# Gathering the sparse rows of a PEER down-projection: from a laid copy, or straight from the weights

## What is computed

```
act = gelu(h . u_table[e])            # for the 128 experts e of the token
w   = softmax gate * act
y   = sum over the 128 picks of  w * v_table[e]
```

## Time and profile before

| | before |
|---|---|
| median of 3 runs | 3961.21 us |
| span of the profiled execution | 3962.2 us |
| TensorE busy | 98% of the span |
| VectorE busy | 72% |
| ScalarE busy | 34% |
| GpSimd busy | 57% |
| granted TensorE clock, mean | 0.998 |

### The profile page before, as it was taken

The page is one execution under the profiler, slowest core; times in us unless marked ns, Lnnn a source line. Parts: engine busy times, 40 slices in busy tenths (PEclk is TensorE's granted clock), DMA queues, the critical chain, the costliest instruction groups (busy, mean ns, idle before and its releaser), DMA issues.

```text
span 3962.2 us, 59722 instructions
## 1 busy us (share of the span) xinstructions
PE 3896.8 (98%) x21569; PEld 3382.9 (85%) x21569; DVE 2842.4 (72%) x3796; ACT 1330.7 (34%) x1577; POOL 2273.4 (57%) x1162
## 2 busy tenths in 40 slices
PE   6999999999999999999999999999999999999998
PEld 5788888888887888888999999999987888888886
DVE  7555555566623459997777777777537999999998
ACT  3233233342213322234444444444323333333332
POOL 6343344434442345446877777788107788787771
PEclk9999999999999999999999999999999999999999
DMA  6555555543442326687888888875549999999994
GB/s 239 189 198 198 198 192 187 194 160 138 159 167 72 117 85 244 234 279 230 243 240 239 239 239 244 245 224 139 192 178 355 375 387 390 383 391 374 391 383 190
DMA packets 385875, 943.27 MB, mean 238 GB/s; under 512 B 104136, under 2 KB 186072, under 8 KB 319736
## 3 DMA queue, kind: packets, MB, share of 16 engines
q1 hardware_dynamic: 177624, 593.08, 41.3%
q0 software_dynamic: 88064, 176.47, 14.2%
q10 hardware_dynamic: 120096, 172.59, 12.6%
HBM read 846.85 MB, written 263.97 MB: 280 GB/s over the span
## 4 chain that ended last, share of the span: by engine, by line
PE 45%; issue 31%; POOL 14%; DVE 7%; DVEq 1%; ACT 1%; DMA 1%; POOLq 1%; SPq 0%; ACTq 0%
POOL wlo L772 13%; PE bank L1670 8%; PE bank L1672 8%; PE bank L1671 8%; PE bank L1728 5%; PE bank L1730 5%; PE bank L1729 5%; DVE wlo L1757 2%; DVE res L2395 2%; PE bank L1389 1%; PE bank L1391 1%; PE bank L1390 1%; ACT whi L1358 1%; DVE res L2414 1%; DVEq L2412 1%
## 5 line engine op out<-in xcount | busy, mean ns | idle before, releaser
L772 POOL TENSOR_TENSOR wlo<-raw,whi 128x1024 fp32r<-128x1024 f32 x296 | 768.7, 2617 | 995.1 <-ACT whi L954 463.6
L834 POOL DMA_INDIRECT gates_d<-sel_g,place_u x384 | 754.9, 1966 | 209.9 <-DMA gates_d<-sel_g,place_u 120.0
L1389 PE MATMUL bank<-h_hi,whi 128*128 128x512 f32 x1712 | 674.4, 394 | 1.9 <-POOL wlo L772 1.3
L1391 PE MATMUL bank<-h_hi,wlo 128*128 128x512 f32 x1712 | 666.9, 390 | 0.0
L1390 PE MATMUL bank<-h_lo,whi 128*128 128x512 f32 x1712 | 666.3, 389 | 0.0
L1728 PE MATMUL bank<-whi,ew_hi 128*128 128x512 f32 x1408 | 550.1, 391 | 14.6 <-DVE wlo L1757 14.6
L1730 PE MATMUL bank<-whi,ew_lo 128*128 128x512 f32 x1408 | 548.5, 390 | 0.0
L1729 PE MATMUL bank<-wlo,ew_hi 128*128 128x512 f32 x1408 | 548.5, 390 | 0.0
L1670 PE MATMUL bank<-h_hi,p_hi 128*128 128x256 f32 x1600 | 452.9, 283 | 0.4 <-DVE p_lo L1757 0.4
L1671 PE MATMUL bank<-h_lo,p_hi 128*128 128x256 f32 x1600 | 452.8, 283 | 0.0
L1672 PE MATMUL bank<-h_hi,p_lo 128*128 128x256 f32 x1600 | 452.8, 283 | 0.0
(11 more groups left out here) (336 smaller groups left out, 7991.9 us busy)
## 6 DMA issues: line engine op xcount, KB each, us to landing
raw<-in_weights SPq DMA_DIRECT2D x338, 1024.0 KB
v_rows_d<-in_weights ACTq DMA_DIRECT2D x96, 1024.0 KB
x_raw<-in_weights SPq DMA_DIRECT2D x50, 1024.0 KB
parts_d<-in_weights SPq DMA_DIRECT2D x32, 1024.0 KB
v_rows_d<-in_weights SPq DMA_DIRECT2D x32, 1024.0 KB
gates_d<-zeros SPq DMA_DIRECT2D x32, 768.0 KB, 10.4
act_d<-mt ACTq DMA_DIRECT2D x128, 192.0 KB
act_in<-act_d SPq DMA_DIRECT2D x64, 384.0 KB
```

What stands on the lines that cost most here:

```text
L772: pool.tensor_tensor(wlo[slot][:, part], raw[slot][:, part], whi[slot][:, part].bitcast(F32), ALU.subtract).then_inc(lo_made, 1)
L834: pool.indirect_dma_start(out=places_d, out_offset=bass.IndirectOffsetOnAxis(ap=place_u[:, t, k:k + 1], axis=0), in_=sel_g[:, t, k:k + 1], ...
L1389: pe.matmul(bank[:, :], whi[slot][:, cols], rhs_hi[:, c, :], start=c == 0, stop=False)
L1391: last = pe.matmul(bank[:, :], wlo[slot][:, cols], rhs_hi[:, c, :], start=False, stop=c == DC - 1)
```

## The change

`parts_d` is dropped. `lay_parts` and its 32 DMAs go, as does the third DMA of `store_acts`. The part rows are gathered from `weights` itself, where the 512 numbers of an expert's quarter lie together; the index table `part_u` is computed to point there. The activations of tile 2 are gathered as single elements from `act_d`, where they lie already for the dense product, by a new `gather_part_act(k)` straight into `w_c[:, k]`, with an index table `pact_u` of its own. `pick_part` goes; `add_part` multiplies `w_c` by the gates once for every 8 picks.

```diff
-        def lay_parts(queue, sbn):
-            queue.dma_start(parts_d[bass.ds(sbn, 1), :, :, 0:512].rearrange("a i p n -> p (a i) n"),
-                            weights[bass.ds(AT_V + 4 * sbn + C_PART, 1), :, :].rearrange("a p (i n) -> (a p) i n", i=4)
-                            ).then_inc(rows_laid, 16)
...
                     if b % 2 == 1:
                         lay_rows(sp, i, b // 2)
-                    else:
-                        lay_parts(sp, 4 * i + b // 2)
...
-            parts = parts_d.rearrange("a i p n -> (a i p) n")
+            parts = weights.rearrange("a p (i n) -> (a p i) n", n=512)
+            part_cells = act_d.rearrange("a p b t -> (a p b t)").unsqueeze(1)
...
+            def gather_part_act(k):
+                pool.indirect_dma_start(out=w_c[:, k:k + 1], out_offset=None, in_=part_cells,
+                                        in_offset=bass.IndirectOffsetOnAxis(ap=pact_u[:, k:k + 1], axis=0)
+                                        ).then_inc(pact_landed, 16)
...
-            pool.wait_ge(rows_laid, 16 * (N_V + SB))
+            pool.wait_ge(rows_laid, 16 * N_V)
...
             for k in range(8):
                 gather_act(k)
+                gather_part_act(k)
...
                     if k % 8 == 0:
                         pool.wait_ge(act_landed, 16 * (k + 8))
+                        pool.wait_ge(pact_landed, 16 * (k + 8))
                     gather_act(k + 8)
+                    gather_part_act(k + 8)
...
-                act.dma_start(parts_d[bass.ds(j, 1), s, :, 512:].rearrange("a p t -> (a p) t"),
-                              mt[s % 2][:, T_PART * P:SD]).then_inc(act_stored[s % 2], 16)
...
+            dve.scalar_tensor_tensor(part_f[:, :], pos_af[:, T_PART, :], float(3 * 4 * P), place_f[:, T_PART, :],
+                                     ALU.mult, ALU.add)
+            dve.drain()
+            dve.tensor_scalar(part_f[:, :], part_f[:, :], float((AT_V + C_PART) * 4 * P), None, ALU.add)
...
-            def pick_part():
-
-                k = len(parts_added)
-                if k == PICKS:
-                    return
-                dve.wait_ge(part_landed[k % ROWS], 16 * (k // ROWS + 1))
-                dve.scalar_tensor_tensor(picked[:, :], part_row[k % ROWS][:, 512:], gate_c[:, k:k + 1], ident[:, :],
-                                         ALU.mult, ALU.mult, accum_out=w_c[:, k:k + 1])
-
             def add_part():
                 k = len(parts_added)
                 if k == PICKS:
                     return
-                dve.drain()
+                if k % 8 == 0:
+                    dve.wait_ge(pact_landed, 16 * (k + 8))
+                    at = slice(k, k + 8)
+                    tt(w_c[:, at], w_c[:, at], gate_c[:, at], ALU.mult)
+                dve.drain()
+                dve.wait_ge(part_landed[k % ROWS], 16 * (k // ROWS + 1))
                 at = res[:, T_PART, 512 * C_PART:512 * (C_PART + 1)]
-                dve.scalar_tensor_tensor(at, part_row[k % ROWS][:, 0:512], w_c[:, k:k + 1], at, ALU.mult, ALU.add
+                dve.scalar_tensor_tensor(at, part_row[k % ROWS][:, :], w_c[:, k:k + 1], at, ALU.mult, ALU.add
                                          ).then_inc(part_used, 1)
```

More of the change, by code:

```diff
@@ L50 @@
 ROW_EXTRA = PART_EXTRA = (1, 3, 4, 6, 7, 9, 10, 12)
-PART_W = 512 + P
 PICKS = RH * TOPK
@@ L271, in build_trunk @@
     place_u = sb("place_u", [P, TD, PICKS], c_at + 18 * kb, U32)
-    part_f = sb("part_f", [P, PICKS], c_at)
+    part_f = sb("part_f", [P, PICKS], c_at + 20 * kb)
     act_in = [sb(f"act_in{k}", [P, 4, SD], a_at + (32 + 12 * k) * kb) for k in range(2)]
@@ L309, in build_trunk @@
     cell_u = w("cell_u", [P, PICKS], 67.5, U32)
+    pact_u = w("pact_u", [P, PICKS], 67, U32)
     gate_p = w("gate_p", [P, PICKS], 68)
@@ L314, in build_trunk @@
     part_u = w("part_u", [P, PICKS], 76.25, U32)
-    part_row = [w(f"part{i}", [P, PART_W], 30 + 2.5 * i) for i in range(ROWS)]
+    part_row = [w(f"part{i}", [P, 512], 30 + 2 * i) for i in range(ROWS)]
     end_hi = whi + [sb("whi2", [P, SL], a_at + 32 * kb, F32R)]
@@ L407, in build_trunk @@
     rows_laid, tables_made = sm("rows_laid"), sm("tables_made")
+    pact_landed = sm("pact_landed")
     act_landed, row_used = sm("act_landed"), sm("row_used")
@@ L641, in _ @@
             for h in range(2):
-                sp.wait_ge(act_stored[h], 48 * 8 + 16)
+                sp.wait_ge(act_stored[h], 32 * 8 + 16)
             sp.wait_ge(prod_done, ALL_PRODUCTS)
@@ L696, in _ @@
             for h in range(2):
-                sp.wait_ge(act_stored[h], 48 * (EB // 2) + 16)
+                sp.wait_ge(act_stored[h], 32 * (EB // 2) + 16)
             for J in range(PAIRS - 2):
@@ L862, in _ @@
             for h in range(2):
-                pool.wait_ge(act_stored[h], 48 * (EB // 2) + 16)
+                pool.wait_ge(act_stored[h], 32 * (EB // 2) + 16)
             for k in range(8):
                 gather_act(k)
+                gather_part_act(k)
             for k in range(PICKS):
@@ L1218, in expert_out @@
                 act.wait_ge(mt_turned, N_Q + 2)
-                act.wait_ge(act_stored[s % 2], 48 * (2 * j + s // 2) + 16)
+                act.wait_ge(act_stored[s % 2], 32 * (2 * j + s // 2) + 16)
                 act.activation(mt[s % 2][:, :], banks[s % 2][:, :], ACT.Gelu_apprx_tanh).then_inc(evac, 1)
@@ L1281, in block_out @@
                 act.wait_ge(outs_added, 14 * g + 7 * h + (21, 20)[i])
-                act.wait_ge(act_stored[i], 48 * (U_PLAIN // 2 + 2 * g + h) + 16)
+                act.wait_ge(act_stored[i], 32 * (U_PLAIN // 2 + 2 * g + h) + 16)
                 act.activation(mt[i][:, :], (c_1, c_2)[i][:, :], ACT.Gelu_apprx_tanh).then_inc(e_made, 1)
@@ L2221, in _ @@
             dve.tensor_copy(gate_c[:, :], sel_g[:, T_PART, :])
-            dve.scalar_tensor_tensor(part_f[:, :], sel_i[:, T_PART, :], float(NK), sel_j[:, T_PART, :], ALU.mult, ALU.add)
             dve.drain()
+            dve.tensor_copy(pact_u[:, :], place_u[:, T_PART, :])
             dve.tensor_copy(part_u[:, :], part_f[:, :]).then_inc(tables_made, 1)
@@ L2429, in _ @@
                     add_row()
-                    pick_part()
                 low_part(J, 1)
```

2 lines of the change are left out of this document (removed).

## The result

The kernel after takes 4122.50 us, median of 4 runs (4117.54 to 4131.57), against 3962.45 us for the kernel before (4 runs, 3960.39 to 3964.01). The ratio is 1.0406, with a 95% interval of 1.0393 to 1.0419: slower by 160 us. The forecast was slower by 111 us, 4073 us, with a range of 4000 to 4150. The direction and the place were foreseen, and the size came out 49 us short.

The account below looks back on a forecast made before the run. TensorE bounds the kernel before; with a fourth gather GpSimd was to bound the down-projection. 3006 us plus 120 picks of 7.9 us, plus issue and landing, puts pick 120 at 3961, 111 us late: 3962.2 + 111 = 4073 us, range 4000 to 4150.

Parts of the forecast that it names:

- the 0.2 us per pick that were put in: GpSimd in the down-projection: waiting for activations to land, once in eight picks, costs 0.2 us per pick (25.3 / 125).
- the 3006 of the sum: Start of the down-projection: with 16 activation gathers in place of 8, the first part gather goes out at 3006 us.
- 2.98 gathers done; the remaining 1.02: Down-projection, per pick: 2.98 gathers at 2.15 us fit in VectorE's 6.6 us of work; 1.02 more cost 1.25 us each.
- 7.9 us per pick: Down-projection: GpSimd's pace with four gathers, 6.6 + 1.3 us, above TensorE's 7.22; limits kept are 7.3 and 8.8.
- two of the signs: Profile after, down-projection: TensorE's waits for `wlo` grow from 14.6 to about 110 us; VectorE's for `row` or `part` 100 to 150.
- the two fast cases: The rivals "GpSimd keeps up" (3947 us, chance 0.08) and "no difference" (3961 us, chance 0.04), left out of the range.
- half of the second: Half of the good-interlocking case: 7.3 us per pick in the down-projection, 4001 us, chance 0.14; the range starts at 4000.
- most of the third's: Most of the case without cheap gathers: 8.8 us per pick in the down-projection, 4181 us, chance 0.11; the range ends at 4150.
- GpSimd keeps up: Rival: GpSimd needs at most 7.22 us per pick in the down-projection, TensorE's 14.6 us of waits come back: 3947 us, chance 0.08.
- no difference: Rival: GpSimd keeps up in the down-projection, TensorE's waits stay as they come from ScalarE's rounding: 3961 us, chance 0.04.
- No cheap gathers: Rival: VectorE's idle time falls where GpSimd waits for activations anyway; 8.8 us per pick in the down-projection, 4181 us, chance 0.11.
- The gathers interlock well: Rival: VectorE's short operations let two gathers through; 7.3 us per pick in the down-projection, 4001 us, chance 0.14.

Follow-up runs that it names:

- e8_laid_copies_back: The kernel after with the 32 laying DMAs and the third activation store put back, unused: 4112.72 us, ratio to the kernel before 1.0377.
- e3_before_plus_gather: The kernel before with one more single-element gather per pick, its result unused: 4127.91 us, ratio to the kernel before 1.0420.
- e9_rows_of_4_kb: The kernel after with row gathers of 1024 numbers in place of 2048, the addition still at full length: 4085.68 us, ratio to the kernel before 1.0308.
- e5_ring_76: The kernel after with GpSimd's descriptor ring at 1216 bytes in place of 1024: 4071.75 us, ratio to the kernel before 1.0275.
- e2_no_fourth_gather: The kernel after without `gather_part_act`, the parts weighted with the gates squared: 3952.96 us, ratio to the kernel before 0.9976.

## Why the prediction came out as it did

**Right: the place and the mechanism.** The stages before 2975 us stayed as they were, the stage's first gather went out at 2974.57, and the laying was worth nothing (`e8_laid_copies_back`). GpSimd became the bound by the fourth gather alone (`e3_before_plus_gather`). Its price is not in the bytes: row gathers of 8 KB and element gathers alike take 0.94 us at their shortest, and rows of half the length leave the mean as it is (`e9_rows_of_4_kb`). VectorE came to wait for rows and TensorE for `wlo`.

**Right with a longer ring, in part by luck: the pace.** The forecast had (7.9 - 0.2) / 4 - 0.30 = 1.63 us for a gather in the mean; the kernel after shows 1.62. I measure the pace from the issue of the first pick's row gather to that of pick 120. In `e5_ring_76` these are 3007.19 and 3952.49 us: 945.3 / 119 = 7.94 us per pick against the forecast 7.9, and 4072 us in all against 4073. The forecast describes a kernel with room in its ring. Some of that closeness is luck. `e5_ring_76` still has some 13 us of ring gaps in mid-stage that no term stood for, 0.1 us per pick, and its waits for activations are 12.6 us, half of the 0.2 us per pick that were put in: the two cancel. Its stage also began 5.5 us before the 3006 of the sum. And the mean of 1.62 us comes from another mix: of the gathers in the stretch of the earlier trace rows 19% took 1 us or less, and the step "2.98 gathers done; the remaining 1.02" makes that about 40% in the new kernel (0.19 x 2.98 + 1.02 = 1.59 of 4), where it shows 31%. The others were shorter than before, 1.94 us in the mean and not 2.07.

In the kernel after the first part gather, at 3003.53, came 2.5 us sooner than said. From the row addition of pick 120, at 4006.15, to the end the kernel after takes 110.9 us, where 112.4 were taken over from the earlier trace rows.

**The term that was mis-sized: "7.9 us per pick" in the sum.** In the kernel after the same two issues are at 3009.30 and 3999.14 us, which is 8.32 us per pick. The step that made it, "In VectorE's 6.6 us of work GpSimd gets (6.6 - 0.2) / 2.15 = 2.98 gathers done; the remaining 1.02 cost 1.25 us each", gives every gather its duration and 0.30 us of issue, and nothing for room. In the trace, from the first part gather (3003.53) to the row addition of pick 120 (4006.15) the kernel after takes 1002.6 us, where the sum had 3961 - 3006 = 955. These 47.6 us, less the 2.5 and some 1.5 by which the start and the end were shorter, are the 44 us by which the profiled execution passed 4073. The other 5.5 us of the 49 are no step of the sum: the median of the four runs lies that far above the profiled execution, which took 4117.0 us. `e5_ring_76` takes 959.1 us between the same two marks (3000.45 and 3959.52), so more room gives back 43.5 of the 47.6. The sign was in the earlier trace rows: I took the gap of 5.2 us for a cost of the start, added it within the 14 us there, and didn't ask for what it waited, nor whether a fourth gather per pick would meet it again in mid-stage, where it came at about every third pick.

**Wrong: two of the signs.** TensorE's waits were to grow to about 110 us as the delay, and 125.8 came with a delay of 155 in the profiled execution. The rest is clock. The windows of the kernel after around its wait of 6.62 us, from 3334.1 to 3340.75 (the last three numbers are granted clock, DMA share, GB/s):

```profile
3332.00:3334.00 2.00, 2.00 (x10) 1.44 (x8) 2.00 (x1) 0.00 (x0) 1.79 (x1) 1.00 0.96 399
...
3336.00:3338.00 2.00, 0.00 (x0) 0.00 (x0) 1.86 (x2) 0.00 (x0) 1.70 (x2) 1.00 0.26 92
3338.00:3340.00 2.00, 0.00 (x0) 0.00 (x0) 2.00 (x2) 0.00 (x0) 1.70 (x2) 0.64 0.00 0
3340.00:3342.00 2.00, 1.25 (x3) 1.06 (x4) 1.93 (x4) 0.00 (x0) 1.70 (x2) 0.50 0.01 0
3342.00:3344.00 2.00, 2.00 (x6) 1.52 (x6) 1.07 (x2) 0.90 (x2) 1.69 (x2) 0.50 0.82 250
...
3346.00:3348.00 2.00, 2.00 (x10) 1.67 (x9) 1.94 (x1) 0.00 (x0) 1.70 (x2) 1.00 0.82 276
```

While TensorE stands still its granted clock falls, and it comes back at 0.50, the lower of its levels (1.2 GHz), with 6 matmuls in 2 us where 10 go at 1.00. In the slice from 3346 it has the upper level (2.4 GHz) again. In the stretch of the down-projection its busy time grew from 888.3 to 931.8 us for one matmul more: 43.5 us. With the waits, 125.8 - 14.6 = 111.2, that is 154.7 us, and the span grew by 4117.0 - 3962.2 = 154.8. The same sum gives 69.4 + 39.4 = 108.8 of 109.0 us in `e5_ring_76`. This is where TensorE spends the delay, not what makes it: that GpSimd would have been no faster with a TensorE at full clock is argued from its never waiting for one in the stretch, and not shown by a run. VectorE's waits for rows, 203.6 us, passed the 100 to 150 said; with the ring of 1216 bytes they are 145.3 us.

One sum of the prediction is off by itself: what its range leaves out (the two fast cases 0.12, half of the second 0.07, most of the third's 0.11) adds to nearly 0.3, not to "about 0.2".

**The rivals.** "GpSimd keeps up" and "no difference" fell: they needed 1.75 us per gather with its issue and got 2.09 (1057 us for 505). "No cheap gathers" fell on the element gathers at 1158 ns. "The gathers interlock well" fell too: it needed 7.3 us per pick, and even with the ring eased it is 7.94. The Trainium skill's remainder of about 115 ns ("SBUF — State Buffer", "A bandwidth-pool intuition that's wrong (but worth ruling out)") was 0.83 us here once more, as at 3332.21. By it there would have been no loss, so the measurement decides.

**The gain from a lighter VectorE**, priced only as part of a rival, is 9.9 us (`e2_no_fourth_gather`), but it needs the activations to come without a fourth instruction in GpSimd's queue. No run found such a way. Of the kernels that leave nothing out, none beats the kernel before by more than 0.2%.

## What to carry to other kernels

An indirect DMA costs GpSimd an instruction, not bytes (here 1.25 us with its issue when VectorE is idle, and 2.15 in the mean beside the busy VectorE of the kernel before), so before one gather is split into two, the queue's time per step of the loop is to be added up and held against the pace of the bound engine: here it had 8% of slack for 33% more gathers. A gap ahead of a gather for which the profile names no releaser, and which ends with the landing of an older one, was a full ring here; such a gap in the kernel before is worth asking what it does in mid-stage at the new rate. The ring's size is then worth a try by itself, in a step large enough for one more gather: 192 bytes gave 51 us back at four gathers per pick, and nothing above 0.2% at three, while with 128 bytes the same gather stood waiting as before. In a full ring the bytes count after all, as they set when a row lands.

## What the runs showed of the hardware

- Room in GpSimd's descriptor ring limits how many gathers may be on their way: with 896, 1024, 1152 and 1216 bytes the first gap comes ahead of the 7th, 8th, 8th and 9th gather of 128 elements. The profile shows the wait as idle time ended by "issue": in the kernel after 4.58 us at the start and 0.5 to 3.4 us in mid-stage, where the plain one is 0.30 us.
- The wait ends 0.52 us after the landing of the row that is four, five, five and six gathers older, for the same four sizes. With rows of 4 KB in place of 8 KB and 1024 bytes it is again the fifth, landed 6.0 us after its gather begins and not 8.1.
- A gather that waits for room thus begins just as VectorE has begun to work on the row that landed, and is held by it: the part gathers take 2311 ns in the mean against 1881 with more room.
- A gather that is held by VectorE ends 0.82 us after VectorE's operation, whichever it is: in the kernel after, 347 gathers under row additions, part additions, `low_part` and the operand products end 0.82 to 0.83 us behind it (5th to 95th percentile). One that isn't held takes 0.94 to 0.96 us, for rows of 8 KB, parts of 2 KB and single elements.
- TensorE's granted clock fell while it stood still from 3334.1 (1.00 in the slice from 3336, 0.64 in the next), stood at 0.50 when its wait of 6.62 us ended at 3340.75, and at 1.00 again in the slice from 3346.
